# The first weight slab with one tile alone, the later slabs one at a time, and the last tile's gating rows written from a copy

## The reference, cut to what matters

```
z = gelu(rms_norm(x) @ w_in);  u, v = split(z)          # 2048 columns each
v = layer_norm(v, ln_g, ln_b)
mixed = einsum('gts,bnsgc->bntgc', tril(w_s), v in chunks of 128 tokens) + b_s
y = (u * mixed) @ w_out;   also returned: the normalised v of the last chunk
```

## Time and profile before

| | us |
|---|---|
| median of 3 runs | 1682.74 (1681.32 to 1683.12) |
| profiled execution, its time | 1676.87 |
| profiled execution, span of the slowest core (core 7) | 1675.3 |
| spans of the eight cores | 1656.4 to 1675.3 |
| PE busy on core 7 | 1616.8 (97%) |
| ACT, DVE, POOL busy on core 7 | 640.7, 724.3, 245.1 |
| data moved by the core's DMA engines | 155.84 MB, mean 93 GB/s |

### The profile page before, as it was taken

One profiled execution on the slowest core, in us unless ns is written; L12 is line 12 of the kernel. 1 busy time (PEld: TensorE's weight loads), 2 busy tenths in 40 slices (PEclk: granted clock), 3 DMA queues, 4 the chain that ended last, 5 costly groups with the idle time before them and its releaser, 6 DMA issues.

```text
span 1675.3 us, 28918 instructions; the slowest of 8 cores (1656.4 to 1675.3 us)
## 1 busy us (share of the span) xinstructions
PE 1616.8 (97%) x10121; PEld 890.1 (53%) x10121; DVE 724.3 (43%) x1362; ACT 640.7 (38%) x1257; POOL 245.1 (15%) x353
## 2 busy tenths in 40 slices
PE   2999999999999999999999899999999999999998
PEld 1457456665456654444444344444445666667643
DVE  2577542223346673111355555333244567622233
ACT  2553441122356672111344335322243677412111
POOL 1232120001112131000112011000012212200000
PEclk8999999999999999999999899999999999999999
DMA  8895275346190186557259873948724505953511
GB/s 173 115 144 76 44 114 76 51 56 84 16 150 1 20 120 105 77 83 119 101 130 152 159 101 62 201 110 155 148 63 74 91 2 78 150 76 55 85 51 53
DMA packets 144338, 155.84 MB, mean 93 GB/s; under 512 B 7410, under 2 KB 137060, under 8 KB 144196
## 3 DMA queue, kind: packets, MB, share of 16 engines
q0 software_dynamic: 116576, 111.47, 46.7%
q1 hardware_dynamic: 27620, 42.53, 8.4%
HBM read 246.89 MB, written 18.55 MB: 158 GB/s over the span
## 4 chain that ended last, share of the span: by engine, by line
PE 89%; DMA 7%; issue 1%; DVE 1%; ACT 1%; POOL 0%; DVEq 0%; POOLq 0%; ACTq 0%; SPq 0%
PE ps L563 87%; DMA t<-sg_w_in 2%; DMA t<-gla_w_in 2%; PE ps L582 2%; DMA sgvp<-t 1%; DMA t<-ffn_w 1%; ACT t L505 1%; DVE t L516 1%; POOL t L539 0%; DVE t L531 0%; DVE t L979 0%; DVE t L792 0%; DVEq L1190 0%; DVEq L1172 0%; DVE t L796 0%
## 5 line engine op out<-in xcount | busy, mean ns | idle before, releaser
L563 PE MATMUL ps<-t,t 128*128 128x512 bf16 (+7 forms) x9353 | 1587.7, 335 | 41.3 <-DMA t<-sg_w_in 20.3
L563 PEld LDWEIGHTS ps<-t,t 128*128 128x128 bf16 (+3 forms) x9353 | 844.9, 99 | 745.1 <-issue 65.8
L505 ACT ACTIVATE t<-ps 128x512 bf16<-128x512 f32 (+5 forms) x719 | 378.8, 537 | 776.4 <-PE ps L563 739.9
L516 DVE TENSOR_TENSOR t<-t,ps 128x512 bf16<-128x512 bf16 (+3 forms) x264 | 131.4, 511 | 425.2 <-PE ps L563 424.1
L516 DVE TENSOR_TENSOR t<-ps,t 128x512 f32<-128x512 f32 (+3 forms) x212 | 176.0, 842 | 273.8 <-PE ps L563 196.9
L539 POOL TENSOR_TENSOR t<-t,t 128x1 f32<-128x1 f32 (+2 forms) x170 | 109.5, 645 | 591.4 <-DVE t L525 294.9
L505 ACT ACTIVATE t<-t 128x1024 bf16<-128x1024 f32 (+3 forms) x153 | 119.3, 781 | 179.1 <-DVE t L531 159.4
L590 POOL DMA_DIRECT2D t<-ffn_w x72 | 63.9, 887 | 571.1 <-PE ps L563 503.7
L505 ACT ACTIVATE t<-t,t 128x1024 bf16<-128x1024 f32 (+2 forms) x76 | 94.7, 1247 | 63.5 <-POOL t L539 59.6
L531 DVE SCALAR_TENSOR_TENSOR t<-t,t,t 128x1024 f32<-128x1024 f32 (+2 forms) x69 | 88.6, 1286 | 41.8 <-POOL t L539 41.4
L531 DVE SCALAR_TENSOR_TENSOR t<-ps,t,t 128x256 bf16<-128x256 f32 (+3 forms) x148 | 79.3, 577 | 30.2 <-PE ps L563 22.7
(11 more groups left out here) (29 smaller groups left out, 130.9 us busy)
## 6 DMA issues: line engine op xcount, KB each, us to landing
t<-ffn_w POOLq DMA_DIRECT2D x56, 1024.0 KB, 12.2
t<-sg_w_in POOLq DMA_DIRECT2D x16, 1024.0 KB, 14.6
t<-gla_w_in POOLq DMA_DIRECT2D x12, 1024.0 KB, 14.4
t<-xp SPq DMA_DIRECT2D x16, 512.0 KB, 5.1
t<-sg_w_out POOLq DMA_DIRECT2D x8, 1024.0 KB, 12.3
t<-st_in SPq DMA_DIRECT2D x64, 128.0 KB, 3.6
sts<-t SPq DMA_DIRECT2D x64, 128.0 KB, 3.7
yp<-t SPq DMA_DIRECT2D x15, 512.0 KB, 2.8
```

The lines of the kernel that those rows point to most:

```text
L505: return e.activation(out=rz(out), in_=rz(in_), func=func, scale=scale, **kw)
L516: return P.op(eng, lambda e: e.tensor_tensor(out=rz(out), in0=rz(a), in1=rz(b), op=op), [a, b], [out], cost, prio=prio, after=after)
L563: ins_ = e.matmul(o, rz(l), rz(r), start=a, stop=b)
```

## The change

At the start, only tile 0 is loaded beside the first slab; tiles 1 to 7 wait until it has landed. The second slab (nb = 1) waits for the power op of tile 4, the third for that of the sample tile and for the second slab, the fourth for the third slab. For the last tile the v rows are first copied into a buffer of their own, `vcp` (4 KB per partition at the very end of the on-chip memory, where `Sch` and `Snb` of the filler also lie), and the four quarters read the copy. Two quarters share one `tmp` buffer, one in each half, and the parts of a pool buffer are now told apart in grains of 64 elements. The planner's rate for slabs goes from 0.29 to 0.25 MB per us, and it adds 2 us to the stores of the quarters.

```diff
     def parts(self):
-        return 1
+        return sum(1 << k for k in range(self.a // 64, (self.b - 1) // 64 + 1))
...
-                    dma_work = max(dma_work, st) + o["nbytes"] / 0.29e6
+                    dma_work = max(dma_work, st) + o["nbytes"] / 0.25e6
...
+    vcp = alloc([128, 16, 128], BF16, [XL - 4096], XL)
...
-    xl.append(load_x(0, 1))
-    for t in range(2, TPS):
+    for t in range(1, TPS):
         xl.append(load_x(0, t, slab_ops[0:1]))
...
-                tr_ = Res("tmp")
-                tq = part(tr_, np_, 0, 512)
-                tq_ = part(tr_, np_, 0, 512, None if np_ == NS else 128)
+                if q % 2 == 0:
+                    tr_ = Res("tmp")
+                o_ = q % 2 * 512
+                tq = part(tr_, np_, o_, o_ + 512)
+                tq_ = part(tr_, np_, o_, o_ + 512, None if np_ == NS else 128)
...
-                store(dst[:, qs], tq, "sgv%d" % (q % 2), np_ * 2048)
+                store(dst[:, qs], tq, "sgv%d" % (q % 2), np_ * 2048, slack=2.0)
...
-                gate = slab_ops[0:1] if nb == 1 else []
+                gate = [[], powers[4:5], powers[8:9] + slab_ops[1:2], slab_ops[2:3]][nb]
...
+                    if last:
+                        copy(vcp[:], v[:, :, colsof(t)])
                     layer_norm(128, t, v[:, :, colsof(t)],
-                               (sgvp, [v[:, q * 4:(q + 1) * 4, colsof(t)] for q in range(4)]) if last else None)
+                               (sgvp, [vcp[:, q * 4:(q + 1) * 4, :] for q in range(4)]) if last else None)
```

More of the change, by code:

```diff
@@ L58, with __init__ @@
 class LV:
-    def __init__(self, bank, n, f32, make):
-        self.bank, self.n, self.f32, self.make = bank, n, f32, make
+    def __init__(self, bank, a, b, f32, make):
+        self.bank, self.a, self.b, self.n, self.f32, self.make = bank, a, b, b - a, f32, make
     def parts(self):
-        return 1
+        return sum(1 << k for k in range(self.a // 64, (self.b - 1) // 64 + 1))
 class Plan:
@@ L700, in make @@
             return v if shape is None else v.rearrange("p (a b) -> p a b", b=shape)
-        return LV(res, b - a, res.kind == "tmp", make)
+        return LV(res, a, b, res.kind == "tmp", make)
     powers = []
@@ L811, in layer_norm @@
                 tt(tq, tq, lbc[0:np_, :], ALU.add)
-                store(dst[:, qs], tq, "sgv%d" % (q % 2), np_ * 2048)
+                store(dst[:, qs], tq, "sgv%d" % (q % 2), np_ * 2048, slack=2.0)
                 if np_ == NS:
-                    t3 = part(tr_, np_, 0, 512, 256)
+                    t3 = part(tr_, np_, o_, o_ + 512, 256)
                     gs = slice(q * 2, q * 2 + 2)
```

## The result

The changed kernel takes **1653.94 us** (median of four, 1652.01 to 1655.84) against 1682.03 before: a ratio of **0.9835, 95% interval 0.9818 to 0.9852**, 28.1 us less. The forecast was 1665.8 with a range of 1656 to 1677, so the direction was right, and more was won than the range allows: the forecast was wrong in its size.

What follows compares the result with a forecast made beforehand. PE bounds the kernel, busy 1616.8 of 1675.3 us; its waits and slow clock can be won. Core 3 as slowest: 1672.9 - 13.5 - 1 = 1658.4, plus 7.4 gives 1665.8, range 1656 to 1677.

Steps and rivals of the forecast that it cites:

- the last term: Whole execution: the median's 7.4 us above the profiled span, carried over unchanged to the new kernel.
- The start, 13.5: First slabs: samples' small products begin at 53.8 instead of 69.2, 15.4 us won, less 1.9 for the clock.
- The clock's 1.9: Start, about 21 to 36 us: PE's pieces partly at 1.2 GHz cost 1.9 us, bounds 0 to 5.5.
- Parts 1 and 2: Start: tile 1's load moved behind slab 1, and gates on slabs 2, 3, 4; together 13.5 us won.
- The reordered rest: Rest of the program: the planner's new slab rate only swaps neighbouring POOL rows; 0, within 3 us either way.
- Core 3's wait: u part: 6.22 us wait ending with ACT stays, power ops behind a slab's issue on POOL; core 3 at 1658.4.
- rival 5: u part: core 3's wait was chance, every core wins as core 7 does; 1661, chance 10%.
- Part 3: u part of pass 1: vcp and pairs of quarters remove store waits; core 7 wins 8 us, bounds 0 and 10.
- 1: Start: PE's pieces all run at 1.2 GHz, so 10 us won there; time 1669.3, chance 15%.
- 2: u part: DVE's wait only moves to lgc and lbc loads and the second store; 1669.2, chance 15%.
- 3: Start: tile loads at 3 us each, PE not fed earlier, some 8 us won; 1671 to 1674, chance 8%.
- 4: Start: slabs one by one can't keep up, PE 15 us late for slab 4; about 1690, chance 3%.

Runs made afterwards that it cites:

- e3: Kernel before with the start's change alone (tile 1's load behind slab 1, slabs 2 to 4 gated one by one): 1670.2 us, ratio 0.9917.
- e14: Kernel after with tile 1's load back beside slab 1, gates of slabs 2 to 4 kept: 1658.6 us, ratio 0.9841.
- e15: Kernel after with the gates of slabs 2 to 4 as before, tile 1 still behind slab 1: 1675.1 us, ratio 0.9945.
- e2: Kernel after with the planner's old slab rate of 0.29e6: 1670.8 us, ratio 0.9922.
- e1: Kernel before with only the planner's slab rate changed, 0.29e6 to 0.25e6: 1677.9 us, ratio 0.9960.
- e9: Kernel after with the old planner rate and slab gates at four places, each behind one more power op or more: 1658.2 us, ratio 0.9859.
- e4: Kernel before with the last tile's change alone (vcp, pairs of quarters, parts, store slack), old rate and start: 1683.2 us, ratio 0.9992.
- e13: Kernel after without the last tile's change (no vcp, quarters one after the other through one buffer): 1668.2 us, ratio 0.9900.
- e11: Kernel after loading only the first half of each weight slab from the ninth on: 1646.6 us, ratio 0.9787.
- e5: Kernel after with the old rate, plus pass 0's fourth u slab gated on the fourth layer-norm power op: 1670.9 us, ratio 0.9918.

## Why the prediction was right, and where it failed

The miss is 11.9 us (1665.8 against 1653.9), and the measured time lies outside the range. 4.0 of them are in the last term: before, the median lay 7.4 above the slowest profiled span, after, 3.4. The time of an execution is about 1.5 us over its slowest span in both; the remaining 5.9 before were the draw of the profiled execution. It took 1676.87, and none of the 55 executions of that kernel behind the experiments' ratios took under 1679.3. So I started from a lucky draw and carried its distance over as fixed; that part of the miss is chance. Whether the spread itself shrinks with the change, as the mean gap in the pairs does (11.4 us before, 6.8 after), is not shown. The other 7.9 are in the span: 1658.4 forecast, 1650.5 found.

- **The start, 13.5: right**, 12.1 us on core 7 by the samples' products, 12.4 to 14.5 at matmul 250, 14.0 by e3. The steps were later than I put them and cancelled: the tiles landed later (the first two squares start at 19.68 and 22.18, forecast landings 18.7 and 20.4), slab 2 issued at 29.8 and not 26.6, landed by 41.8 and not 37.1, PE through with slab 1 at 43 and not 39.6; against that, next to nothing was lost behind it. Slab 2's sum has 1 us "for the completion" that no run shows; from issue to landing it took 11.4 us where the sum has 10.5. ACT set the pace, as said. The clock's 1.9 was too much: 16 matmuls took 4.31 at 27.01 instead of 3.56, so 0.8, and all later ones ran at the full clock. The 0.70 from which I argued is a mean: from 27 to 45 us before, the granted clock was 0.53. Parts 1 and 2 were not alike: e14 gives tile 1's load nothing, e15 gives the gates all.
- **A rule against the gates** (the Trainium skill, "DMA: Bandwidth & Descriptors", section "Rules for kernel authors": issue early, wait late) would have them cost time. e15 shows them worth 19 us here, so in this case the measurement goes against the rule. Two things differ from the rule's picture, and no run separates them: the DMA engines are full, and the issue that waits stands on POOL, where others need the ops behind it.
- **The reordered rest, "0, within 3 us": the step that failed.** The term was put at 0 and measured 15 us on top of the other two parts (e2) and 7 alone (e1), outside its bounds of 3 either way. The prediction itself had the mechanism, in its first section: power ops that stand on POOL behind the issue of a slab. I applied it to the start, saw the swaps of neighbouring rows on POOL, and did not ask which neighbours: a power op of half a microsecond and an issue that may stand 5 to 13 us. Nor was it POOL alone: the new rate also changes the lists of PE, ACT and DVE in many places, and what that is worth is not known beyond the 4 us between e9 and after.
- **Core 3's wait**: "the new list still has a slab's issue ahead of them" was true of that list, and the wait was still there, but 2.42 instead of 6.22 us. I read an order where a landing decided; rival 5 (the wait was chance, and every core wins) came nearest, at 1661.
- **Part 3, 8 us on core 7: right in size there** (11.7 between matmuls 5200 and 5800, with PE's waits of 5.12 and 2.67 and the clock's loss gone). The copy took 0.63 us beside PE's work. On this core there is one wait on a store, as said, 1.58; the loads of `sg_ln_g` and `sg_ln_b` then keep DVE for 4.16 and 3.25, which PE doesn't feel. Wrong was to take it as a matter of core 7 alone, and to add it up: alone it is nothing (e4), beside the new rate 11 (e13).
- **Rivals.** 1 fell (clock 0.85, not 0.70), though its "none above 5" was wrong: PE waits 6.11 us at 24.52. 2 fell on core 7 but not on the cores that set the time: core 0 waits 6.38 us for a store of `sgvp` and PE 3.76 behind it, and a wait of the old length there was one of the prediction's own signs of being wrong. So part 3 holds on core 7 and only in part on cores 0 and 3. 3 and 4 fell: slab 2 took 11.4 us, under 14.

What stays open: why landings are late on one core of a pair. The traces show only that they are (in e2, and in the kernel before by 0.7 to 1.0 us in the mean in each pair), not whether that makes the core late or comes of it, and in after it does not hold for the pair 0/1. Also the 4 us between e9 and after, and how much of e13's 11 us is a loss of the new list.

## What to carry to other kernels

On an engine that issues DMAs and computes, price a swap of an issue and an op by looking up how long the issue stands in the trace, on the latest core, and not by the op. That wait is only an upper bound: here the issues stood up to 13 us, one place put right alone won nothing, and four together 10.6 us. When two waits can each set the time of the same late core, taking one away may show nothing: remove both, or test each in the presence of the other fix. Read the spans of all cores before picking the one to reason from, and start from the median of several executions and not from the profiled one, which may be a lucky draw.

## What the runs showed of the hardware

- **When one of cores 2k and 2k+1 is late, the other is early.** In 15 executions of the kernel before, their spans differ by 11.4 us in the mean, against 8.3 and 8.0 for two other pairings within the die, with a correlation of −0.36 against 0.00 and 0.06 (mean of four pairs each); in e2 20.6 us and −0.74. In the three executions of e13 the gap is 8.7 us, against 7.5 and 7.4, so it does not show in every set. With half the bytes (e11) the gap is 2.7. The Trainium skill, "HBM Reference", section "Specifications (TRN2)", says that the two cores of a pair share the bandwidth of one HBM domain; these runs agree with that, though none of them isolates it or shows that 2k and 2k+1 are such a pair.
- **A small lag at the start can stand beside a large one at the end.** In e5 core 6 gets to the samples' first products at 57.51 us and core 7 at 55.48; they end at 1665.8 and 1641.9, with the same instructions in the same order. Between them lie core 6's waits of 3.24, 7.80 and 1.61 us at the places above, which core 7 does not have.
